# First modulation block of a transformer step loaded and used in two halves by channels, with products of the first projections set between the halves

## What is computed

```python
cs = jax.nn.silu(c)
sh1, sc1, gt1, sh2, sc2, gt2 = jnp.split(cs @ w_ada[i] + b_ada[i], 6, axis=-1)
h = ada_modulate(rms_norm(x, g_mix[i]), sh1, sc1)      # h * (1 + sc1) + sh1
...
q, k, v, qi, ki, wi = split_cols(h @ w_in, A_WIDTHS)   # layer 0: indexed sparse attention
```

## Time and profile before

| | us |
|---|---|
| median of 3 runs | 1578.24 |
| lowest and highest | 1576.38, 1578.61 |
| the profiled execution | 1578.52 |
| its span in the trace | 1576.7 |
| PE busy | 1523.8 |
| DVE, ACT, POOL busy | 1028.0, 639.9, 564.5 |

### The profile page before, as it was taken

The page is one execution under the profiler, slowest core; times in us unless marked ns, Lnnn a source line. Parts: engine busy times, 40 slices in busy tenths (PEclk is TensorE's granted clock), DMA queues, the critical chain, the costliest instruction groups (busy, mean ns, idle before and its releaser), DMA issues.

```text
span 1576.7 us, 29451 instructions
## 1 busy us (share of the span) xinstructions
PE 1523.8 (97%) x11530; PEld 1386.7 (88%) x11530; DVE 1028.0 (65%) x2034; ACT 639.9 (41%) x1280; POOL 564.5 (36%) x347
## 2 busy tenths in 40 slices
PE   4999999999999999999999999999899999999997
PEld 2868856899999999999888888886899999999997
DVE  1559866558886778855644544556687876688734
ACT  3434365334552145522533333334254541355324
POOL 1124922124761066621322222221127640376410
PEclk8999999999999999999999999999999999999998
DMA  9784400232254432452254444443331355333421
GB/s 338 252 292 142 127 11 2 69 106 68 81 144 154 143 83 82 117 163 70 65 172 124 126 127 130 131 124 102 126 102 54 90 171 162 88 93 101 134 74 60
DMA packets 244454, 189.22 MB, mean 120 GB/s; under 512 B 12888, under 2 KB 228608, under 8 KB 240112
## 3 DMA queue, kind: packets, MB, share of 16 engines
q1 hardware_dynamic: 231520, 179.13, 37.9%
q10 hardware_dynamic: 12816, 8.44, 1.7%
HBM read 175.44 MB, written 8.50 MB: 117 GB/s over the span
## 4 chain that ended last, share of the span: by engine, by line
PE 87%; ACT 4%; DVE 3%; POOL 3%; issue 2%; DMA 1%; ACTq 0%; SPq 0%; DVEq 0%; POOLq 0%
PE lin L820 38%; PE lin L1340 27%; PE lin L837 5%; PE S L1116 2%; PE O L1165 1%; PE O L1234 1%; PE O L905 1%; PE T L1145 1%; POOL w_lo L2052 1%; DVE acc_out L2554 1%; PE S L993 1%; PE S L1187 1%; DMA ada_raw<-in_w_ada 1%; PE S L1035 1%; PE T L1202 1%
## 5 line engine op out<-in xcount | busy, mean ns | idle before, releaser
L2052 POOL TENSOR_TENSOR w_lo<-w_raw,w_hi 128x1024 fp32r<-128x1024 f32 (+3 forms) x68 | 168.1, 2475 | 423.9 <-ACT w_hi L1528 423.9
L2148 POOL TENSOR_TENSOR w_lo<-ada_raw,w_hi 128x512 fp32r<-128x512 f32 x114 | 157.7, 1386 | 246.3 <-ACT w_hi L1818 246.3
L1528 ACT ACTIVATE w_hi<-w_raw 128x1024 fp32r<-128x1024 f32 (+2 forms) x110 | 124.7, 1134 | 120.5 <-PE lin L820 104.0
L820 PE MATMUL lin<-act_hi,w_hi 128*128 128x288 f32 (+1 forms) x1088 | 165.7, 304 | 5.5 <-ACT act_hi L1560 2.0
L820 PE MATMUL lin<-act_hi,w_lo 128*128 128x288 f32 (+1 forms) x1088 | 168.1, 300 | 0.2
L820 PEld LDWEIGHTS lin<-act_hi,w_hi 128*128 128x128 f32 (+1 forms) x1088 | 151.0, 191 | 17.3 <-issue 12.3
L820 PE MATMUL lin<-act_lo,w_hi 128*128 128x288 f32 (+1 forms) x1088 | 162.5, 298 | 0.0
L820 PEld LDWEIGHTS lin<-act_hi,w_lo 128*128 128x128 f32 (+1 forms) x1088 | 151.0, 189 | 7.6 <-issue 6.7
L820 PEld LDWEIGHTS lin<-act_lo,w_hi 128*128 128x128 f32 (+1 forms) x1088 | 150.3, 188 | 3.4 <-issue 2.9
L2148 POOL TENSOR_TENSOR w_lo<-s_tmp,w_hi 128x512 fp32r<-128x512 f32 x76 | 128.9, 1716 | 14.6 <-ACT w_hi L1821 14.6
L1340 PE MATMUL lin<-act_hi,w_hi 128*128 128x288 f32 x608 | 105.3, 295 | 0.0
(11 more groups left out here) (327 smaller groups left out, 3051.5 us busy)
## 6 DMA issues: line engine op xcount, KB each, us to landing
ada_raw<-in_w_ffn_in SPq DMA_DIRECT2D x76, 512.0 KB, 5.2
w_raw<-in_w_ffn_out SPq DMA_DIRECT2D x32, 704.0 KB, 4.9
ada_raw<-in_w_ada SPq DMA_DIRECT2D x20, 1024.0 KB, 7.7
ada_raw<-in_w_ada SPq DMA_DIRECT2D x32, 512.0 KB, 5.1
w_raw<-in_w_in_b SPq DMA_DIRECT2D x32, 512.0 KB, 4.2
w_raw<-in_w_in_a SPq DMA_DIRECT2D x16, 512.0 KB, 5.3
ada_qo<-in_w_ada SPq DMA_DIRECT2D x8, 1024.0 KB, 7.2
ada_raw<-in_w_ada_final SPq DMA_DIRECT2D x16, 512.0 KB, 5.7
```

The source lines that it names most:

```text
L820: last = nc.tensor.matmul(lin_u(u)[0:m, tok], w, (lo if p == 2 else hi)[:, at(t) if at else t, tok], start=(p == 0 and t == 0), stop=(p == ...
L1528: A(w_hi[:, u % 2, 0:n], w_raw[:, u % 2, 0:n], ACT.Copy).then_inc(whi_done, 1)
L2052: TT(w_lo[:, u % 2, 0:n], w_raw[:, u % 2, 0:n], w_hi[:, u % 2, 0:n].bitcast(F32), ALU.subtract)\
L2148: TT(ring(w_lo, q), raw, ring(w_hi, q).bitcast(F32), ALU.subtract).then_inc(ws_lo_p, 1)
```

## The change

Block 0 is divided by channels: half h holds, of the shift and of the scale, the 512 channels of kt 4h to 4h+3. Each load brings 128 rows x (2 pieces of 512 columns), 512 KB in pieces of 2 KB, and there are 16 loads and 16 steps, of two matmuls each. Half 0 writes partitions 0 to 31 and 64 to 95 of O, half 1 the other two groups.

- PE: eight steps of half 0, spread of rstd, transposes, products of U_KIW and U_QI over kt 0 to 3 (`first_pair(0)`: for each kt the first kind of both, then the second and the third kind of each), eight steps of half 1, transposes, cache index keys, `first_pair(1)`.
- ACT: two copies of O for half 0, with the splits of w_raw behind them; one copy (partitions 32 to 63) for half 1, between act_hi of kt 3 and kt 4.
- DVE: for half 1 a copy of partitions 96 to 127; for each half bias, multiplier, four fo, four act_lo. POOL clears ada_row at the start, and clears permb later: behind the first two splits, when all 16 steps are done.
- SP: eight loads of half 0, w_raw of U_KIW and U_QI, eight loads of half 1 (the last four wait for steps 1 to 4 of half 0, whose slots they take), the rest as before. `ada_used` counts steps of half 1 alone in this block.

```diff
+            def ada0_load(h, kt):
+
+                if h == 1 and kt >= 4:
+                    sp.wait_ge(ada0_used, kt - 3)
+                cols = ada_src(0, kt)[:, :].rearrange("r (j h c) -> r j h c", j=2, h=2)[:, :, h, :]
+                sp.dma_start(ada0_slot(h, kt).rearrange("p (j c) -> p j c", j=2), cols).then_inc(ada0_in[h][kt], 16)
+
             for kt in range(KT):
-                if kt >= 6:
-                    sp.wait_ge(ada_used, kt - 5)
-                sp.dma_start(ada0_slot(kt), ada_src(0, kt)).then_inc(ada0_in[kt], 16)
+                ada0_load(0, kt)
...
             qi_load(0)
+            for kt in range(KT):
+                ada0_load(1, kt)
...
-            def after_norm(u, m, base):
-
-                for kt in range(KT):
-                    lin_part(u, None, KT, m, act_hi, act_lo, ready=split_ready(base), some=[(0, kt)])
+            def first_pair(h):
+
+                u, kts = U_KIW, range(4 * h, 4 * h + 4)
+                for kt in kts:
+                    lin_part(u, None, KT, 72, act_hi, act_lo, ready=split_ready(ACT_N0), some=[(0, kt)])
                     lin_part(u + 1, None, KT, P, act_hi, act_lo, some=[(0, kt)])
-                for p, v, cols in ((1, u, m), (1, u + 1, P), (2, u, m), (2, u + 1, P)):
-                    lin_part(v, 3 + p, KT, cols, act_hi, act_lo, ready=split_ready(base) if v == u else None)
+                for p in (1, 2):
+                    lin_part(u, None, KT, 72, act_hi, act_lo, ready=split_ready(ACT_N0), some=[(p, kt) for kt in kts])
+                    lin_part(u + 1, None, KT, P, act_hi, act_lo, some=[(p, kt) for kt in kts])
...
+            def ada0_step(h, kt):
+
+                pe.wait_ge(ada0_in[h][kt], 16)
+                for j in range(2):
+                    c = 64 * j + 32 * h
+                    last = nc.tensor.matmul(O[c:c + 32, 0:512], cs_w[:, kt, :],
+                                            ada0_slot(h, kt)[:, 512 * j:512 * j + 512],
+                                            start=(kt == 0), stop=(kt == KT - 1))
+                last.then_inc(ada_used if h else ada0_used, 1)
...
             pe.wait_ge(cs_done, 1)
-            for kt in range(3):
-                ada_step(kt)
+            for kt in range(KT):
+                ada0_step(0, kt)
             norm_spread(0)
-            for kt in range(3, KT):
-                ada_step(kt)
-            ada_transpose(0, T_ADA0)
+            ada0_transpose(0)
+            first_pair(0)
+            for kt in range(KT):
+                ada0_step(1, kt)
+            ada0_transpose(1)
             cache_index_keys()
...
-            after_norm(U_KIW, 72, ACT_N0)
+            first_pair(1)
             linear(U_QI + 1)
...
-                ada_evac(0)
+                act.wait_ge(ada0_used, KT)
+                act.wait_ge(ada_zero, 1)
+                A(ada_row[0:32, :], O[0:32, :], ACT.Copy)
+                A(ada_row[64:96, :], O[64:96, :], ACT.Copy).then_inc(ada0_low, 1)
                 split_hi(U_KIW, KT * 72)
                 split_hi(U_QI, N)
                 for kt in range(KT):
+                    if kt == 4:
+                        act.wait_ge(ada_used, KT)
+                        A(ada_row[32:64, :], O[32:64, :], ACT.Copy).then_inc(ada_row_done, 1)
                     act.wait_ge(y_done, kt + 1)
...
-            pool.wait_ge(ada_used, 5)
-            nc.gpsimd.memset(permb[:, :, :], 0.0).then_inc(perm_zero, 1)
...
             split_lo(U_KIW, KT * 72)
             split_lo(U_QI, N)
+            pool.wait_ge(ada_used, KT)
+            nc.gpsimd.memset(permb[:, :, :], 0.0).then_inc(perm_zero, 1)
             split_lo(U_QI + 1, N)
...
+                for h in range(2):
+                    if h == 1:
+                        dve.wait_ge(ada_used, KT)
+                        dve.wait_ge(t_ready, T_ADA0 + 1)
+                        V.tensor_copy(ada_row[96:128, :], O[96:128, :]).then_inc(ada0_top, 1)
...
+                    for kt in range(k0, k0 + 4):
+                        for c0, c1, st, r in parts:
+                            last = scale_part(0, kt, c0, c1, st, r)
+                        last.then_inc(y_done, 1)
+                    for kt in range(k0, k0 + 4):
+                        dve.wait_ge(acthi_done, ACT_N0 + kt + 1)
+                        for c0, c1, st, _ in parts:
+                            last = low_part(0, kt, c0, c1, st)
+                        last.then_inc(act_ready, 1)
```

More of the change, by code:

```diff
@@ L183, in last_sum @@
     return max(k for k in range(end) if k % 4 // 2 == slot)
-T_ROWS, T_ADA0, T_KIC, T_KIW, T_KC, T_ADA1 = 0, 2, 3, 4, 5, 7
-T_K0, T_V0 = 8, 12
-T_ADA2 = 16
-T_A = 17
+T_ROWS, T_ADA0, T_KIC, T_KIW, T_KC, T_ADA1 = 0, 2, 4, 5, 6, 8
+T_K0, T_V0 = 9, 13
+T_ADA2 = 17
+T_A = 18
 T_ADA3 = T_A + 4 * PAIRS
@@ L427, in encoder_step @@
         lin_free = [sem("lin_free0"), sem("lin_free1")]
-        ada0_in = [sem(f"ada0_in{kt}") for kt in range(KT)]
+        ada0_in = [[sem(f"ada0_in{h}_{kt}") for kt in range(KT)] for h in range(2)]
+        ada0_used, ada0_low, ada0_top = sem("ada0_used"), sem("ada0_low"), sem("ada0_top")
+        ada_zero = sem("ada_zero")
         ada_in = [sem(f"ada_in{n}") for n in range(4)]
@@ L897, in ada_step @@
                 b, kt = n // KT, n % KT
-                if b == 0:
-                    pe.wait_ge(ada0_in[kt], 16)
-                else:
-                    pe.wait_ge(ada_in[n % 4], 16 * ((n - KT) // 4 + 1))
-                if kt == 0 and b >= 1:
+                pe.wait_ge(ada_in[n % 4], 16 * ((n - KT) // 4 + 1))
+                if kt == 0:
                     pe.wait_ge(ada_row_done, b)
@@ L905, in ada_step, with ada0_transpose @@
                     last = nc.tensor.matmul(O[32 * j:32 * j + 32, 0:512], cs_w[:, kt, :],
-                                            (ada0_slot(kt) if b == 0 else ada_slot(n))[:, 512 * j:512 * j + 512],
+                                            ada_slot(n)[:, 512 * j:512 * j + 512],
                                             start=(kt == 0), stop=(kt == KT - 1))
                 last.then_inc(ada_used, 1)
+            def ada0_step(h, kt):
[6 more added lines that the diff above has]
+                last.then_inc(ada_used if h else ada0_used, 1)
+            def ada0_transpose(h):
+                if h == 0:
+                    pe.wait_ge(ada0_low, 1)
+                else:
+                    pe.wait_ge(ada_row_done, 1)
+                    pe.wait_ge(ada0_top, 1)
+                t_use(T_ADA0 + h)
+                for c in range(4):
+                    last = nc.tensor.transpose(T[:, c * P:(c + 1) * P], ada_row[:, c * P:(c + 1) * P], ident)
+                last.then_inc(t_ready, 1)
             def sum_collect(hb):
@@ L2056, in _ @@
             nc.gpsimd.memset(ones[:, :], 1.0).then_inc(ones_done, 1)
+            nc.gpsimd.memset(ada_row[:, :], 0.0).then_inc(ada_zero, 1)
             nc.gpsimd.memset(eps[:, :], EPS).then_inc(ones_done, 1)
@@ L2269, in norm0 @@
                 V.reciprocal(rstd[:, :], root[:, 0:5]).then_inc(rstd_done, 1)
-                ada_mods(0, T_ADA0)
-                multiplier(0, T_ADA0)
-                dve.wait_ge(rstd_spread, 1)
                 parts = ((0, NP_, 0, S[:, 1, :]), SAMPLE)
-                for kt in range(KT):
-                    for c0, c1, st, r in parts:
-                        last = scale_part(0, kt, c0, c1, st, r)
-                    last.then_inc(y_done, 1)
-                for kt in range(KT):
-                    dve.wait_ge(acthi_done, ACT_N0 + kt + 1)
-                    for c0, c1, st, _ in parts:
-                        last = low_part(0, kt, c0, c1, st)
-                    last.then_inc(act_ready, 1)
+                for h in range(2):
[3 more added lines that the diff above has]
+                        V.tensor_copy(ada_row[96:128, :], O[96:128, :]).then_inc(ada0_top, 1)
+                    t = T_ADA0 + h
+                    dve.wait_ge(t_ready, t + 1)
+                    V.tensor_tensor(mods[:, 0:16, :].rearrange("p (j h c) s -> p j h c s", j=2, h=2)[:, :, h, :, :],
+                                    T[:, :].rearrange("p (c j h s) -> p j h c s", c=4, j=2, h=2)[:, :, h, :, 0:2],
+                                    vecs[:, 0:16].rearrange("p (j h c a) -> p j h c a", j=2, h=2, a=1)[:, :, h, :, :]
+                                    .broadcast_to([P, 2, 4, 2]), ALU.add).then_inc(t_free, 1)
+                    dve.wait_ge(t_free, t + 1)
+                    k0 = 4 * h
+                    V.scalar_tensor_tensor(mulA[:, 0, k0:k0 + 4, :], mods[:, SCALE[0] + k0:SCALE[0] + k0 + 4, :], 1.0,
+                                           gains[:, GAIN[0] + k0:GAIN[0] + k0 + 4].rearrange("p (k a) -> p k a", a=1)
+                                           .broadcast_to([P, 4, 2]), ALU.add, ALU.mult).then_inc(muls_step, 1)
+                    muls[0] += 1
+                    dve.wait_ge(muls_step, muls[0])
+                    dve.wait_ge(rstd_spread, 1)
+                    for kt in range(k0, k0 + 4):
```

(1 more changed line is left out.)

10 lines of the change are left out of this document (7 added, 3 removed).

## The result

The changed kernel takes **1587.27 us** (median of 4 runs, 1586.26 to 1587.81) beside 1578.42 of the kernel before (4 runs, 1576.38 to 1579.85): ratio 1.0056, 95% interval 1.0039 to 1.0074. It is 8.85 us slower. The direction was forecast, the size wasn't: 1582.6 was said, and 1586 was the upper end. The profiled execution took 1586.26, with a span of 1584.5, 7.8 longer than the span of before.

A forecast was written before the change was run, and what follows sets the result against it. PE, busy 97% of the span, was taken to bound the kernel, so the third projection's delay carries to the end: 2.35 plus 2.0 for the clock is 4.35 us, giving 1582.6 us; range 1578.5 to 1586.

The forecast's parts named there:

- Items 1 and 3: First half on PE: eight half steps at 0.92 us each, loads hidden; then products, 3.1 us and 4.3 us.
- Rival A: Half steps cost half, 0.49 us each; total 1576.7 us, not slower than before; chance 10%.
- Item 2: First half's copy, transposes and small operations: steps end at 24.1, first product at 29.0; small operations no larger than before.
- Item 4: Second half: loads land by 34, steps end at 43.7, first product at 48.1, products end at 55.5.
- Item 5: Third projection starts 2.4 us after ACT begins its split, at 56.8, 2.35 us later than 54.48.
- item 6: Clock halves behind two PE gaps, near 25.9 to 29.0 and 45.1 to 48.1: 1.0 us each, 2.0 together.
- the bare 2.35: Delay in us of the third projection's start with everything at full clock, before the clock's 2.0 is added.
- item 7: SP's load queue moves from 34.15 to 43.7; third projection's weights land by 54.2, wanted 54.4; later loads covered, no cost.
- The clock term: Cost of half clock behind the two PE gaps ahead of each half's first products: 2.0 us together.
- Rival B: Clock stays up through both PE gaps; total 1580.6 us; chance 15%.
- Rival C: Third projection's weights come 1 to 3 us late; total 1583.6 to 1585.6 us, say 1584.6; chance 15%.
- Rivals D and E: D: a wait puts first products behind second half's steps, 1586.6 us, 3%. E: half loads don't overlap, 1597 us, 2%.

The follow-up runs named there:

- e9: Kernel before, with the steps of modulation blocks 1 and 2 doing two of their four matmuls: 1580.42 us, ratio 1.0007.
- e11: The changed kernel run again, unaltered, with a profile: 1588.47 us, ratio 1.0063 to the kernel before.
- e5: Changed kernel with third and fourth projection weights loaded earlier and both PE gaps filled with idle matmuls: 1580.41 us, ratio 1.0010 to the kernel before.
- e2: Changed kernel with the third and fourth projection weights issued ahead of SP's wait for the last half step: 1585.4 us, ratio 1.0048 to the kernel before.
- e7: Changed kernel with PE's order altered, half 1's steps ahead of half 0's products: 1577.99 us, ratio 0.9991 to the kernel before.
- e12: Kernel before, with POOL's first split waiting for DVE's multiplier: 1576.93 us, ratio 0.9988.
- e4: Changed kernel with idle matmuls filling both PE gaps ahead of each half's first products: 1583.77 us, ratio 1.0039 to the kernel before.
- e10: Kernel before, with idle matmuls between steps that wait for loads and behind the transposes: 1578.78 us, ratio 1.0000.
- e3: Changed kernel with POOL's split of the fourth projection's weights waiting until DVE has made the index keys: 1591.15 us, ratio 1.0076 to the kernel before.
- e8: e7 plus early weight loads, POOL's first split behind the multiplier, and U_KIW's products ahead of U_QI's in half 1: 1576.03 us, ratio 0.9980 to the kernel before.
- e6: Kernel before, with each block 0 load cut into two of 512 KB in 2 KB pieces: 1579.36 us, ratio 1.0006.

## Why the prediction was wrong in size

- *Items 1 and 3, steps and the two halves of products*: right. Half steps went in 0.88 each, predicted 0.92; loads never held them; products took 7.9 and 8.6 with the falling clock, predicted 8.4 each (7.4 and 1.0). Rival A, half steps at half price, is refuted by the 0.88 and by e9.
- *Item 2, to the first product*: 5.55 for 4.9. The multiplier took 1.26 beside POOL's split. In before it took 0.65 under the same neighbour, and half 1 had 0.17 with POOL idle; I had written "no larger than before". Item 4 had 4.4 for this way and it took 3.9, so the two offset each other.
- *Item 5 and item 6, as far as the third projection*: 41.64 from the first step, 3.89 more than before; predicted 4.35 (2.35 and 2.0 for the clock). e11 has 5.18. With the clock up (e5) it is 2.42 for the bare 2.35. To this point the sum was sound, and some of that is luck: in e5 the way to the first product is 0.7 longer than item 2 had it and the end 0.4, the two runs of half steps are 0.3 shorter each and item 4's way 0.5.
- **The step that failed is item 7**, and in it the sentence that each later load is issued as long after SP's point as now, "and all of them before the swap of rows", from which I took them to be covered. With it fell the premise that what the third projection loses is what the kernel loses. The issue was as written (10.7 behind the last step before, 10.85 after); what was never asked is when the *next* load, of U_QI+2, lands and who wants it. It lands at 63.05, ACT wants it at 60.1, its split drives POOL's, and POOL's split hits DVE's rotation: 1.03 + 0.43 of waits and 1.6 of half clock, 3.1 of the 3.24; 2.65 in e11. I took 0. Undoing this alone (e2) brings the stretch to 13.73. The rows themselves I had allowed to land 2 us late, as PE wants them 8 us after; they landed 1.0 late, and with DVE's operations between them and PE only 2.05 of delay were free.
- *The clock term* was 2.0 and measured 1.5 (change) and 2.8 (e11), beside e5. With both repairs 7.5 of the 8.85 came back, and the bare 2.35 lies within what is left.
- *What item 7 doesn't explain*: the miss is 8.85 - 4.35 = 4.5. Item 7 makes 3.24 of it in the trace, the way to the third projection takes back 0.46, and 1.7 (1.9 in e11) appears in the medians alone.
- Rival B (clock stays up) didn't occur. Rival C, late weights of the *third* projection, didn't occur by 0.9 us (landed 56.1, wanted 57.03), and did as soon as the gaps were filled. I had the right mechanism one load too early. Rivals D and E didn't occur.
- *Why the change loses at all*, shown by e7: the order, with steps that cost as much by half as whole. The loads of half 1 have landed while PE still does the products of half 0, so its 7.0 us of steps, and the copy and transposes behind them, are covered by nothing; before, all steps but the last were covered by loads.

Open: what takes e12's other 1.5 us, where the change loses the 1.7 us that its head doesn't show, why e4 gains more in the median than in its trace, and why one and the same kernel varies by some 2 us behind the mark.

## What to carry to other kernels

Before you halve a tiled step, ask which dimension of the engine's array the halves leave empty: here halving the output groups halved the matmuls and not the time, so PE's steps went from 7 or 8 us to 14. Work that waits for loads belongs ahead of work that doesn't, where the loads can cover it; put the other way round, and with the half clock and the late loads that followed, the same instructions cost some 10 us. When a queue's starting point moves by 10 us, follow *every* transfer of the list to its user, and then what that user starts: the damage came through a neighbour that nobody waited for, and it showed only where the slack was used up.

## What the runs showed of the hardware

- **A matmul step costs the same with two column groups of four as with all four**: 0.88 (two, change) and 0.87 (four, e10 and e12) for steps in a row, 0.98 and 1.00 between products (e9 and before).
- **POOL beside DVE.** An operation of DVE with two inputs from SBUF took 2.78 to 2.91 us instead of about 0.75 while POOL did w_lo = w_raw - w_hi (change, e3, e4, e11). The excess is near what is left of the POOL operation, which takes 2.4 in all: in the change POOL's ran from 64.25 to 66.64, and DVE's, begun at 64.41, ended at 67.25. With 1.68, 1.31, 0.76 and 0.41 us of POOL's left, DVE's took 2.29 (e7), 1.92 (e5), 1.38 (e12) and 1.01 (e2). That the multiplier took 0.65 before and 1.26 after is then what was left of POOL's operation when it came. Where DVE was first it was POOL's that grew: 2.98 in e4. The operations for fo, with S from PSUM, took 3.49 for eight beside POOL's splits (change, half 0) and the same with POOL idle (e8, half 1). The Trainium skill (SBUF — State Buffer, section Who interferes with whom) says that a VectorE instruction with two SBUF inputs and a GpSimd instruction that reads SBUF shut each other out, and that the one issued first keeps the port for its whole length; all of these numbers agree.
- **The clock fell at waits of 3.62 and 1.67 us (the second with short transposes ahead of it), not behind the 1.56 ahead of the third projection, and once more behind a run of small transposes with waits of 1.03 and 0.43** (third fall; in e11 with 0.53 and 0.43). At one and the same wait it fell at different moments: at the wait of 3.62, which ran to 30.54 in the change and to 29.65 in e11, it fell at about 30.3 and 27.7. It stayed at half for about 3 us in the change and 7 in e11, and so the same two gaps cost 1.5 us in one execution and 2.8 in another. In none of the gaps that were filled (e4's two, e5, e10) did it fall.
- **Half clock costs little where loads or ACT set the pace.** In the kernel before, 30 to 44 us, taking it away (e10) changed nothing that the medians show (0.9990 to 1.0009), and 0.9 to 1.3 us in the trace.
- Loads of 512 KB in 2 KB pieces flowed at 385 to 388 GB/s, loads of 1024 KB in 8 KB pieces at 416 to 426 (e6 and before, 16 to 28 us). The kernel's time didn't show it: ratio 1.0006, 0.9997 to 1.0016.
